# Moving one projection unit of the next head behind two transposes of the current head in a latent-attention block (streaming encoder, one Trainium2 core)

## What is computed

```
def _expand_latent(c, w_ukv, g_knope):
    kv = jnp.einsum('bsc,chd->bshd', c, w_ukv)
    kn = _rms_norm(kv[..., :QK_NOPE_DIM], g_knope)
    return kn, kv[..., QK_NOPE_DIM:]

def _mla_block(qn, qr, qpos, kn, kr, v, kpos):
    logits = (jnp.einsum('bqhd,bkhd->bhqk', qn, kn, preferred_element_type=jnp.float32)
              + jnp.einsum('bqhr,bkr->bhqk', qr, kr, preferred_element_type=jnp.float32)) * MLA_SCALE
    mask = (kpos // CHUNK)[None, :] <= (qpos // CHUNK)[:, None]
    p = jax.nn.softmax(jnp.where(mask, logits, NEG_INF), axis=-1)
    return jnp.einsum('bhqk,bkhd->bqhd', p.astype(v.dtype), v)
```

## Time and profile before

| what | us |
|---|---|
| median of 3 runs | 2146.37 |
| the profiled execution | 2145.84 |
| its span in the trace | 2144.1 |
| PE busy | 2133.9 |
| DVE busy | 1213.3 |
| ACT busy | 995.8 |
| POOL busy | 249.7 |

### The profile page before, as it was taken

One profiled execution on the slowest core, in us unless ns is written; L12 is line 12 of the kernel. 1 busy time (PEld: TensorE's weight loads), 2 busy tenths in 40 slices (PEclk: granted clock), 3 DMA queues, 4 the chain that ended last, 5 costly groups with the idle time before them and its releaser, 6 DMA issues.

```text
span 2144.1 us, 33654 instructions
## 1 busy us (share of the span) xinstructions
PE 2133.9 (100%) x11609; PEld 1870.8 (87%) x11609; DVE 1213.3 (57%) x2781; ACT 995.8 (46%) x2287; POOL 249.7 (12%) x261
## 2 busy tenths in 40 slices
PE   9999999999999999999999999999999999999999
PEld 7888888888888888888888988888899999998899
DVE  6555554545555555556223344443467777777986
ACT  5544444434444444453223433443366666665433
POOL 1000000000000000000000001421332001021011
PEclk9999999999999999999999999999999999999999
DMA  5333333333233333333442333343332212122451
GB/s 185 107 104 114 105 104 89 114 109 98 94 105 104 104 110 108 104 101 115 146 136 80 112 100 94 122 137 122 127 102 83 57 50 64 50 67 90 153 172 63
DMA packets 127462, 225.30 MB, mean 105 GB/s; under 512 B 21104, under 2 KB 75120, under 8 KB 127264
## 3 DMA queue, kind: packets, MB, share of 16 engines
q1 hardware_dynamic: 127392, 224.36, 33.4%
HBM read 191.42 MB, written 32.89 MB: 105 GB/s over the span
## 4 chain that ended last, share of the span: by engine, by line
PE 94%; DVE 3%; ACT 1%; issue 1%; DMA 1%; POOL 0%; SPq 0%; ACTq 0%; DVEq 0%; POOLq 0%
PE bank L214 67%; PE bank L2653 8%; PE bank L2004 4%; PE bank L961 1%; PE bank L937 1%; PE bank L2709 1%; PE bank L2687 1%; PE bank L2703 1%; PE bank L953 1%; PE bank L1997 1%; PE bank L2689 1%; PE bank L929 1%; PE bank L2681 1%; PE bank L271 0%; DVE h_tlo L1882 0%
## 5 line engine op out<-in xcount | busy, mean ns | idle before, releaser
L214 PE MATMUL bank<-b_whi,x_hi 128*128 128x512 f32 x1016 | 401.4, 395 | 0.2
L214 PE MATMUL bank<-b_whi,x_lo 128*128 128x512 f32 x1016 | 396.5, 390 | 0.0
L214 PE MATMUL bank<-b_wlo,x_hi 128*128 128x512 f32 x1016 | 396.5, 390 | 0.0
L197 DVE SCALAR_TENSOR_TENSOR b_wlo<-b_raw,first,b_whi 128x512 fp32r<-128x512 f32 x254 | 179.4, 747 | 140.8 <-ACT b_whi L184 139.8
L184 ACT ACTIVATE b_whi<-b_raw,first 128x512 fp32r<-128x512 f32 x254 | 169.4, 715 | 160.2 <-PE bank L214 133.1
L214 PEld LDWEIGHTS bank<-b_whi,x_lo 128*128 128x128 f32 x1016 | 190.7, 188 | 40.8
L214 PEld LDWEIGHTS bank<-b_whi,x_hi 128*128 128x128 f32 x1016 | 191.0, 188 | 36.6 <-DVE b_wlo L197 0.8
L214 PEld LDWEIGHTS bank<-b_wlo,x_hi 128*128 128x128 f32 x1016 | 191.0, 188 | 35.3
L214 PE MATMUL bank<-m_whi,x_hi 128*128 128x512 f32 x320 | 125.0, 391 | 0.0
L214 PE MATMUL bank<-m_wlo,x_hi 128*128 128x512 f32 x320 | 124.6, 389 | 0.0
L214 PE MATMUL bank<-m_whi,x_lo 128*128 128x512 f32 x320 | 124.6, 389 | 0.0
(11 more groups left out here) (547 smaller groups left out, 5362.9 us busy)
## 6 DMA issues: line engine op xcount, KB each, us to landing
b_raw<-w_fox SPq DMA_DIRECT2D x127, 512.0 KB, 3.5
m_raw<-w_mla SPq DMA_DIRECT2D x40, 512.0 KB, 3.5
c_raw<-w_out SPq DMA_DIRECT2D x32, 512.0 KB, 3.5
h_ring<-w_out2s SPq DMA_DIRECT2D x16, 768.0 KB, 6.0
f_raw<-w_ukv SPq DMA_DIRECT2D x16, 512.0 KB, 3.6
queries<-e_q SPq DMA_DIRECT2D x16, 480.0 KB, 4.5
e_raw<-w_uq SPq DMA_DIRECT2D x32, 192.0 KB, 2.5
f_qa<-queries SPq DMA_DIRECT2D x16, 320.0 KB, 3.7
```

The source lines that it names most:

```text
L197: op = eng.scalar_tensor_tensor(lo[:, k, :], raw[:, k, :], self.gain[:, K:K + 1], hi32[:, k, :], ALU.mult, ALU.subtract)
L214: op = eng.matmul(out, a, w[:, k, :], start=(first and k == 0 and i == 0), stop=(last and k == self.kk - 1 and i == len(pairs) - 1))
```

## The change

In `ORDER`, the name T5 moves from behind `p3` to behind `p2`. `pn` and `p2`, which stood behind T5, now follow `p3` directly. `JOBS` has no T names in it and stays as it is, so every bank and every semaphore count is unchanged. `FINAL` is written out separately and does not change. In `FIRST` the names qr and qn stay tied to T5.

```
     ORDER = ["kp", "T0", "T1", "s3", "ka", "T2", "s2", "new", "T3", "s1", "s0", "T8", "sa", "sb", "T4",
-             "p3", "T5", "pn", "p2", "p1", "T6", "on", "p0", "g", "T7", "ont", "qr", "qn", "o"]
+             "p3", "pn", "p2", "T5", "p1", "T6", "on", "p0", "g", "T7", "ont", "qr", "qn", "o"]
```

## The result

| | before | after |
|---|---|---|
| median, us | 2146.10 (4 runs) | 2163.84 (4 runs, 2163.25 to 2164.18) |
| the profiled execution, us | 2145.84 | 2163.25 |
| its span, us | 2144.1 | 2161.5 |
| PE busy, us | 2133.9 | 2134.0 |

The ratio of after to before is 1.0082, with a 95% interval of 1.0070 to 1.0094: slower by 17.7 us. The forecast was 2164.0. (A fourth run of the kernel before has moved its median from 2146.37 to 2146.10.) PE does the same work in the same time; what was added is time in which it stands still.

A forecast was written before the change was run, and what follows sets the result against it. PE's row of matmuls was taken to bound the kernel. 15 x 1.44 = 21.6 us for pn's wait, less 3.9 for p1's, makes +17.7 us: a median of 2164.0 us, 8-in-10 range 2159.0 to 2168.5.

The forecast's parts named there:

- What bounds the kernel: Whole kernel: PE's row of matmuls bounds it, busy 2133.9 us of a span of 2144.1.
- Step 1: PE at pn: without T5's cover it waits 1.44 us per head for the release by ACT's samples' Exps.
- The bound of 0.1 us: pn's start out of a pause: uncertain by 0.1 us either side of 1.44, or 1.5 us over 15 heads.
- The sign that the distance from p3's start to pn's would be about 1.55 us: PE between p3 and pn: the distance of starts grows to about 1.55 us with no matmul in it.
- Step 2: PE at p1: T5 now covers its wait for p3's low part, a gain of 3.9 us, 0.26 per head.
- Step 3: ACT and DVE behind T5: late squares and p1's parts still leave g 0.8 us to spare, costing nothing.
- Step 4: T6 through the next head's kp: all comes as much later as PE does, at no further cost or gain.
- The sum: Over 15 heads: 21.6 us less 3.9 makes +17.7 us, or 1.18 per head; median 2164.0 us.
- pn is ready in time: Rival at pn: it follows p3 at once and only p1's gain is left, -3.9 us, 2142.5; chance 0.03.
- the stall is absorbed: Rival: ACT and DVE set the pace, within 4 us of 2146.4, chance 0.03; partly absorbed, +6 to +13 us, 0.05.
- The granted clock: Rival: PE's clock falls to 1.2 GHz behind each pause, another 34 us, 2198; chance 0.02.
- A second wait behind the first: Rival: g's reserve is used up and PE waits again, 0.5 us per head, 7.5 us more, 2171.5; chance 0.05.

The follow-up runs named there:

- The quarter: The change, but 9 of T5's 12 matmuls stay behind p3 and 3 go behind p2; 2147.20 us, ratio to before 1.0006.
- the half: The change, but 6 of T5's 12 matmuls stay behind p3 and 6 go behind p2; 2152.48 us, ratio to before 1.0031.
- the dose table: Kernels with 3, 6 or all 12 of T5's matmuls moved behind p2, against the kernel before: +1.2, +6.5 and +17.7 us measured.
- the edit that looked like a gain of 3 us: On the kernel before, DVE's three small rates instructions go behind p3's low part in place of ahead of it; 2152.40 us, ratio 1.0030.
- a neighbour of it: On the kernel before, two rates instructions go behind p3's low part and two of the gate's five scalings behind p2's low part; 2143.01 us, ratio 0.9987.

## Why the prediction was right

*What bounds the kernel.* Confirmed by PE's busy time, equal to 0.1 us while the span grew by 17.4.

*Step 1, pn's wait, 1.44 us per head.* The mechanism is shown by the runs: the wait is pn's alone (2163.83 with T5 ahead of p2), it grows with the part of T5 taken away, and it ends with ACT's Exps. The size is slightly off: 1.38 us and not 1.44. PE was through with p3 at 1699.08 + 0.107 = 1699.19 and pn started at 1700.52, which is 1.33 us; the other 0.05 stand between pn's first and second transpose. The prediction took pn's start as it was in a stream, 0.11 us behind its weight load; out of a pause the row of the matmul starts 0.01 behind it. The bound of 0.1 us that was put there for this reason holds it. The sign that the distance from p3's start to pn's would be about 1.55 us did not come: it is 1.44.

*Step 2, p1's wait gone, 3.9 us.* The mechanism is confirmed: its row is gone, and the rates' order, which makes p3's low part earlier, changes nothing in the change (2164.02). The size was a little too large. The 0.26 us a head are the idle time of the weight load; in PE's starts the wait cost 0.23 us, 3.5 in all. The quarter and the half agree: their passes grew by 0.08 and 0.43 us, by the new pause less this term.

*Step 3, T5's squares and p1's high part at no cost.* Confirmed: g has 0.88 us to spare, forecast 0.8, both counted to g's matmul. The method was good enough for so large a reserve. In the expectation for T6 ahead of p1 it was not: g's lateness was read 0.11 us too small, and the next follower was not looked at.

*Step 4, all that follows at no cost.* The irregular waits are the same rows with the same numbers, and the stage behind the last `ka` is as long as before (2161.5 - 1958.7 = 202.8 us; 2144.1 - 1941.3 = 202.8).

*The sum.* 1.16 us per head, forecast 1.18; 15 of it are 17.4 us, as the two profiled executions differ (2163.25 - 2145.84 = 17.4), and the medians by 17.7. That the forecast came within 0.2 us of the median is in part luck: both terms were too large, by 0.06 and 0.03 us a head, and one is taken from the other.

*The rivals.* That pn is ready in time is refuted by its wait. That the stall is absorbed is refuted by the dose table: already the half comes through in full. The granted clock is 1.00 in every stretch, with a pause of PE of more than 1.3 us in each 24.3, and behind the pause T5's matmuls keep their distance of 0.12 us (1701.24, 1701.36, 1701.48). The Trainium skill ("TensorE: Matmul & The Clock Gate", section "A second HAM failure mode: psum-queue depth-cycling") tells of a kernel whose clock swung with frequent short idle times between groups of matmuls; this trace, with one pause per head, shows no such swing. A second wait behind the first did not arise.

## What to carry to other kernels

Where a full engine works through a fixed order, ask of each piece of work whose wait it covers; to move it cost here its length, as far as the cover was needed, and one look at what ends just when the piece ends told how far. Count the waits it covers in the new place against that: here 0.23 us against 1.38 per head. To move a few tenths of small work on another engine, follow that engine's queue up to the next three waiters: the edit that looked like a gain of 3 us cost 6.5, and a neighbour of it gained 2.9.

## What was not expected

A matmul out of a pause starts sooner behind its weight load than one in a stream (0.01 us in the row, against 0.11), but the one behind it comes later (0.16 us, against 0.11 between transposes). So a pause costs 0.05 us less than the cover that was taken away: 1.38 us against 1.44. An Exp that sums its row holds its release back by the read-out behind it: without the sums, pn's wait ended 0.31 us earlier per head for two Exps.
